# Gates of the prompt's HGRN group: worked out on the projection's tiles instead of in the recurrence's stage

## What is computed

```python
q = silu(q_raw)
log_f = logaddexp(log1p(-lb) + log_sigmoid(f_raw), log(max(lb, 1e-30)))
k = (1 - lb) * sigmoid(-f_raw)
# in chunks, per head, with the state S (64 x 64):
b = cumsum(log_f, axis=time)
attn[t, s] = sum_k q[t, k] * k[s, k] * exp(b[t, k] - b[s, k])      # s <= t
o = attn @ v + (q * exp(b)) @ S
S = exp(b_last)[:, None] * S + (k * exp(b_last - b)).T @ v
out = rms(o) * gain * silu(g_raw)
```

## Time and profile before

| what | value |
|---|---|
| three runs | 4513.45, 4522.64, 4520.75 us, median 4520.75 |
| span of the profiled execution | 4510.9 us |
| least time of a run beside that span | 4513.45 us, 2.55 more |
| TensorE busy | 3762.7 us, 83% |
| VectorE busy | 1959.3 us, 43% |
| ScalarE busy | 1491.7 us, 33% |
| GpSimd busy | 588.2 us, 13% |

### The profile page before, as it was taken

The page is one execution under the profiler, slowest core; times in us unless marked ns, Lnnn a source line. Parts: engine busy times, 40 slices in busy tenths (PEclk is TensorE's granted clock), DMA queues, the critical chain, the costliest instruction groups (busy, mean ns, idle before and its releaser), DMA issues. The chain is left out here.

```text
span 4510.9 us, 50016 instructions
## 1 busy us (share of the span) xinstructions
PE 3762.7 (83%) x18532; PEld 2697.6 (60%) x18532; DVE 1959.3 (43%) x2982; ACT 1491.7 (33%) x2438; POOL 588.2 (13%) x908
## 2 busy tenths in 40 slices
PE   8999965899995664577559986769999999999997
PEld 6778843655562552342324444458788788788875
DVE  4122135877764776332213325533453443443333
ACT  3122123344444544121102214332432343343232
POOL 2001001354555000212010100000000000000000
PEclk9999965999998677687579987789999999999998
DMA  4233222111111001635153302643343233333222
GB/s 148 88 98 121 77 58 67 49 45 31 43 29 66 6 29 59 212 121 180 40 170 103 100 28 69 216 158 94 108 135 103 100 118 118 108 112 103 75 75 77
DMA packets 260783, 421.46 MB, mean 93 GB/s; under 512 B 48291, under 2 KB 150034, under 8 KB 259090
## 3 DMA queue, kind: packets, MB, share of 16 engines
q1 hardware_dynamic: 216054, 293.06, 20.3%
q0 software_dynamic: 35248, 119.86, 8.1%
q10 hardware_dynamic: 9248, 5.46, 0.4%
HBM read 335.89 MB, written 84.50 MB: 93 GB/s over the span
## 5 line engine op out<-in xcount | busy, mean ns | idle before, releaser
L2970 PE MATMUL ff_p<-ff_h,ff_wl 128*128 128x512 f32 x1024 | 403.1, 394 | 30.6 <-DVE ff_wl L3178 23.5
L3178 DVE TENSOR_TENSOR ff_wl<-ff_w_raw,ff_w 128x2048 fp32r<-128x2048 f32 x128 | 293.4, 2292 | 309.9 <-ACT ff_w L3066 309.0
L3031 PE MATMUL ff_p<-ff_w,ff_yl 128*128 128x512 f32 x1024 | 404.1, 395 | 11.3 <-DVE ff_yl L3188 9.6
L3031 PE MATMUL ff_p<-ff_wl,ff_yh 128*128 128x512 f32 x1024 | 401.2, 392 | 0.0
L2970 PE MATMUL ff_p<-ff_hl,ff_w 128*128 128x512 f32 x1024 | 400.8, 391 | 0.0
L3031 PE MATMUL ff_p<-ff_w,ff_yh 128*128 128x512 f32 x1024 | 400.7, 391 | 0.0
L2970 PE MATMUL ff_p<-ff_h,ff_w 128*128 128x512 f32 x1024 | 400.7, 391 | 0.0
L1490 ACT ACTIVATE att_e<-att_p 128x512 f32<-128x512 f32 (+3 forms) x432 | 205.1, 509 | 311.5 <-PE att_p L1378 308.2
L3066 ACT ACTIVATE ff_w<-ff_w_raw 128x2048 fp32r<-128x2048 f32 x128 | 244.6, 1911 | 150.5 <-PE ff_p L3031 113.0
L1542 DVE TENSOR_REDUCE att_mx<-att_p 128x1 f32<-128x512 f32 (+3 forms) x432 | 230.0, 571 | 85.4 <-PE att_p L1409 60.7
L3188 DVE TENSOR_TENSOR ff_yl<-ff_y,ff_yh 128x512 fp32r<-128x512 f32 x256 | 171.4, 689 | 199.6 <-ACT ff_yh L3080 199.6
(11 more groups left out here) (726 smaller groups left out, 7068.0 us busy)
## 6 DMA issues: line engine op xcount, KB each, us to landing
ff_w_raw<-in_w_ff SPq DMA_DIRECT2D x128, 1024.0 KB, 5.3
att_raw<-scratch_feat SPq DMA_DIRECT2D x72, 256.0 KB, 4.2
scratch_feat<-proj_f SPq DMA_DIRECT2D x68, 256.0 KB, 2.0
smp_fox_kv<-in_cache_fox_kv SPq DMA_DIRECT2D x64, 256.0 KB, 5.4
smp_fox_kv<-in_cache_fox_kv POOLq DMA_DIRECT2D x64, 256.0 KB, 5.7
proj_w_raw<-in_w_in POOLq DMA_DIRECT2D x24, 512.0 KB, 4.1
proj_w_raw<-in_w_in POOLq DMA_DIRECT2D x40, 256.0 KB, 4.0
proj_x<-in_x_prompt POOLq DMA_DIRECT2D x16, 512.0 KB, 4.3
```

What stands on the lines that cost most here:

```text
L2970: last = mm(p[:, bank, :], lhs(a, c), b[:, c, :], start=(c == 0 and a is wl), stop=(c == KC - 1 and a is w and b is h))
L3031: last = mm(bank, a[:, v % NY, cols], b[:, U % 2, o:o + 512], start=(q == 0 and s == 0 and a is yl), stop=(q == UB - 1 and s == 3 and a is ...
L3178: v_.tensor_tensor(wl[:, U % 2, :], w_raw[:, U % 2, :], w[:, U % 2, :].bitcast(F32), ALU.subtract).then_inc(w_lo, 1)
```

## The change

The gate work of the prompt moves from the HGRN stage into the projection. Each evicted tile of q, f and g goes through it while it lies in `f`: `gate_first` and `gate_second` on ScalarE, `gate_logs` and `gate_make` on VectorE, the latter two steps one unit later. A tile of f is stored twice, as running sums in a new scratch tensor `hgrn_b` and as k in `feat`; q and g are stored as gated rows. The lower bounds are made in the projection's first units. `squares` gives its place to the new tiles; the squares now go into `xn`, so `norm` waits for an earlier turn. In the HGRN stage the gates go, `b` becomes a ring of four blocks and is loaded, ahead of the gated rows. `Steps` and `lower_bounds` only move up in the file. The diff, cut to the core:

```diff
--- before.py
+++ after.py
@@ stage_project, tiles
-        squares = r.sb("squares", [P, D])
+        ga, gb, once = r.sb("ga", [P, GA, TB]), r.sb("gb", [P, 2, TB]), r.sb("once", [P, TB])
...
@@ SyncE
+            def store_gated(u):
...
+                sp.wait_ge(g_made, n + 1)
+                if what == "f":
+                    sp.dma_start(S["hgrn_b"][c * P:(c + 1) * P, at], f[:, f_use[u] % 4, :]).then_inc(f_stored[f_use[u] % 4], 16)
+                    sp.dma_start(S["feat"][R_HF + c * P:R_HF + (c + 1) * P, at], ga[:, n % GA, :]).then_inc(k_stored[n % GA], 16)
+                else:
+                    row = {"q": R_HQ, "g": R_HG}[what] + c * P
+                    sp.dma_start(S["feat"][row:row + P, at], f[:, f_use[u] % 4, :]).then_inc(f_stored[f_use[u] % 4], 16)
...
-                elif kind == "feat":
+                elif kind == "feat" and u not in gates:
...
                 if u and u - 1 in tr_use:
                     store_turned(u - 1)
+                if u - 1 in gates:
+                    store_gated(u - 1)
@@ ScalarE
+                    act.wait_ge(turned, n - 1)
-                s.activation(squares[0:rows, :], x[0:rows, n % 3, :], ACT.Square, accum_out=ss[0:rows, k]).then_inc(ss_done, 1)
+                s.activation(xn[0:rows, n % 2, :], x[0:rows, n % 3, :], ACT.Square, accum_out=ss[0:rows, k]).then_inc(ss_done, 1)
...
+            def gate_first(u):
+                n, what, c = gates[u]
+                act.wait_ge(out_done, u + 1)
+                if n >= GA:
+                    act.wait_ge(g_made, n - GA + 1)
+                    act.wait_ge(k_stored[n % GA], k_before(n))
+                a = ga[:, n % GA, :]
+                gstep(s.activation(a, f[:, f_use[u] % 4, :], ACT.Abs))
+                gstep(s.activation(a, a, ACT.Exp, scale=-1.0))
+                s.activation(a, a, ACT.Ln, bias=1.0).then_inc(g_first, 1)
+
+            def gate_second(u):
+                n, what, c = gates[u]
+                a, t = ga[:, n % GA, :], f[:, f_use[u] % 4, :]
+                act.wait_ge(g_logs, n + 1)
+                if what == "f":
+                    gstep(s.activation(t, t, ACT.Abs))
+                    gstep(s.activation(t, t, ACT.Exp, scale=-1.0))
+                    gstep(s.activation(t, t, ACT.Ln, bias=1.0))
+                s.activation(a, a, ACT.Exp).then_inc(g_second, 1)
...
                 out(u)
...
+                if u - 1 in gates:
+                    gate_second(u - 1)
+                if u in gates:
+                    gate_first(u)
@@ VectorE
+            def gate_logs(u):
...
+                dve.wait_ge(g_first, n + 1)
+                gstep(v.scalar_tensor_tensor(out=a, in0=t, scalar=0.0, in1=a, op0=ALU.min, op1=ALU.subtract))
+                if what == "f":
+                    gstep(v.tensor_scalar(gb[:, c, :], a, lb["ln_om"][:, c:c + 1], None, ALU.add))
+                    gstep(v.tensor_tensor(a, a, t, ALU.subtract))
+                    gstep(v.tensor_scalar(t, gb[:, c, :], lb["ln_lb"][:, c:c + 1], None, ALU.subtract))
+                dve.sem_inc(g_logs, 1)
+            def gate_make(u):
...
+                dve.wait_ge(g_second, n + 1)
+                if what == "q":
+                    gstep(v.tensor_tensor(t, t, a, ALU.mult))
+                elif what == "g":
+                    gstep(v.scalar_tensor_tensor(out=t, in0=t, scalar=ggain[:, c:c + 1], in1=a, op0=ALU.mult, op1=ALU.mult))
+                else:
+                    v.tensor_scalar(a, a, lb["one_minus"][:, c:c + 1], None, ALU.mult)
+                    gstep(v.scalar_tensor_tensor(out=t, in0=gb[:, c, :], scalar=lb["ln_lb"][:, c:c + 1], in1=t, op0=ALU.max,
+                                                 op1=ALU.add))
+                    gstep(v.tensor_tensor_scan(t, once[:], t, 0.0, ALU.mult, ALU.add))
+                dve.sem_inc(g_made, 1)
...
+                if u - 1 in gates:
+                    gate_make(u - 1)
+                if u in gates:
+                    gate_logs(u)
@@ stage_hgrn
-        b, eb = r.sb("b", [P, 2, 2, TB]), r.sb("eb", [P, 2, 2, TB])
+        b, eb = r.sb("b", [P, 4, 2, TB]), r.sb("eb", [P, 2, 2, TB])
...
+                sp.dma_start(b[:, k % 4, :, :], S["hgrn_b"][:, at].rearrange("(c p) t -> p c t", p=P)).then_inc(b_loaded[k % 4], 16)
...
-            def gate_sigmoids(k):
...
-            def gate_forget(k):
...
-                act.wait_ge(scanned, k + 1)
+                act.wait_ge(b_loaded[k % 4], 16 * (k // 4 + 1))
...
-            def gate_logs(k):
...
-            def gate_scan(k):
...
+                dve.wait_ge(b_loaded[(j // PER) % 4], 16 * (j // PER // 4 + 1))
...
+                dve.wait_ge(z_loaded[k % 4], 48 * (k // 4 + 1))
```

More of the change, by code:

```diff
@@ L175, in _, with __init__, __call__, closed @@
             nc.vector.memset(K["pairones"][HD:P, HD:P], 1.0)
+class Steps:
+    def __init__(self, engine, sem, i=0, per=0):
+        self.engine, self.sem, self.start, self.per, self.n = engine, sem, i * per, per, 0
+    def __call__(self, instruction):
+        self.n += 1
+        instruction.then_inc(self.sem, 1)
+        self.engine.wait_ge(self.sem, self.start + self.n)
+    def closed(self, instruction, passed):
+        self(instruction)
+        self.engine.sem_inc(passed, 1)
+    def end(self):
+        assert self.per == self.n, (self.per, self.n)
 HALF = L // 2
@@ L199, with lower_bounds @@
 PROJ_TURN = {0: ((0, R_FK, P), (P, R_FK + P, P)), 1: ((256, R_CMP, P), (384, R_KS, HD))}
+def lower_bounds(nc, step, low, lb):
+    v = nc.vector
+    return [
+        lambda: step(v.tensor_tensor(lb["shift"][:], low[:], low[:], ALU.subtract)),
+        lambda: step(v.reciprocal(lb["inv"][:], lb["exp"][:])),
+        lambda: step(v.tensor_tensor(lb["soft"][:], lb["exp"][:], lb["inv"][:], ALU.mult)),
+        lambda: step(v.tensor_tensor(lb["lb"][:], lb["soft"][:], lb["soft"][:], ALU.subtract)),
+        lambda: step(v.tensor_scalar(lb["one_minus"][:], lb["lb"][:], -1.0, 1.0, ALU.mult, ALU.add)),
+        lambda: step(v.tensor_single_scalar(lb["floored"][:], lb["lb"][:], 1e-30, ALU.max)),
+    ]
+LN2_60 = 60 * 0.6931471805599453
+GATED = {R_HQ + P * c: ("q", c) for c in range(2)} | {R_HF + P * c: ("f", c) for c in range(2)} | {
+    R_HG + P * c: ("g", c) for c in range(2)}
 def proj_units():
@@ L282, in stage_project, with k_before @@
         sm_stored = r.sems("sm_stored", 2)
+        g_consts, bounds_dve, bounds_act, gate_dve, gate_act = (r.sem(n) for n in (
+            "g_consts", "bounds_dve", "bounds_act", "gate_dve", "gate_act"))
+        g_first, g_logs, g_second, g_made, k_stored = (
+            *(r.sem(n) for n in ("g_first", "g_logs", "g_second", "g_made")), r.sems("k_stored", GA))
         block = r.block()
+        gates = {}
+        for u, (hf, g, kind, a, b) in enumerate(units):
+            if kind == "feat" and PROJ_ROWS[g][a][0] in GATED:
+                gates[u] = (len(gates), *GATED[PROJ_ROWS[g][a][0]])
+        def k_before(n):
+            return 16 * sum(kind == "f" and m % GA == n % GA and m < n for m, kind, _ in gates.values())
         z_use, f_use, zs_use, tr_use, fs_use, sm_use = {}, {}, {}, {}, {}, {}
@@ L430, in _ @@
                     store_turned(u - 1)
+                if u - 1 in gates:
+                    store_gated(u - 1)
+            for k in range(GA):
+                sp.wait_ge(k_stored[k], 16 * sum(kind == "f" and n % GA == k for n, kind, _ in gates.values()))
             for k in range(3):
@@ L616, in _ @@
                     finish_small(u)
+                if u == 1:
+                    dve.wait_ge(g_consts, 32)
+                    low_bounds[0]()
+                    dve.sem_inc(bounds_dve, 1)
+                    ones = once[:].rearrange("p (n t) -> p n t", t=P)
+                    v.memset(ones[:, :, 1:P], 1.0)
+                    v.memset(ones[:, :, 0:1], 0.0)
+                if u == 3:
+                    dve.wait_ge(bounds_act, 1)
+                    for bound in low_bounds[1:]:
+                        bound()
+                    dve.sem_inc(bounds_dve, 1)
+                if u == 5:
+                    dve.wait_ge(bounds_act, 2)
+                    gstep(v.tensor_scalar(lb["ln_lb"][:], lb["ln_lb"][:], LN2_60, None, ALU.subtract))
+                if u - 1 in gates:
+                    gate_make(u - 1)
+                if u in gates:
+                    gate_logs(u)
             for u in (NU - 2, NU - 1):
@@ L723, in _ @@
             turn_out(NU - 1)
-class Steps:
-    def __init__(self, engine, sem, i=0, per=0):
-        self.engine, self.sem, self.start, self.per, self.n = engine, sem, i * per, per, 0
-    def __call__(self, instruction):
-        self.n += 1
-        instruction.then_inc(self.sem, 1)
-        self.engine.wait_ge(self.sem, self.start + self.n)
-    def closed(self, instruction, passed):
-        self(instruction)
-        self.engine.sem_inc(passed, 1)
-    def end(self):
-        assert self.per == self.n, (self.per, self.n)
 def split(v, step, x, high, low):
```

134 lines of the change are left out of this document (31 added, 103 removed).

## The result

Four runs of the changed kernel took 4417.04 to 4428.64 us, median 4424.22, against 4519.56 for four of the kernel before: a ratio of 0.978, 95% interval 0.977 to 0.980, some 95 us less. The forecast was 4430 us in a range of 4412 to 4463. The profiled execution spans 4415.4 us, 95.5 less than the one before.

What follows compares the result with a forecast made beforehand. It took TensorE to bound the projection and a chain of waits across engines, no single engine, the HGRN stage. Opening 30.7 plus chunks 60.3, projection 0, gave 91.0 us less: 4430 us, range 4412 to 4463.

Steps and rivals of the forecast that it cites:

- The opening: Start of the HGRN stage: without block 0's gates the first factors start earlier, a gain of 30.7 us.
- the overlap of VectorE and GpSimd: HGRN opening: VectorE's differences slowed beside GpSimd's selects, 5.6 of eight done by 1432.9, cutting the gain from 32.4 to 30.7.
- the first rival: HGRN opening: GpSimd's selects wait for differences too; opening gain 29.0, total 89.3, 4431.5 us; chance 0.36.
- the sum without contention: HGRN opening undisturbed: exponentials end at 1435.4, masks last at 1436.05, a gain of 32.4 us.
- The chunks: HGRN chunks: without later gates, 13 steps of 11.87 us take 154.3 against 214.6, a gain of 60.3 us.
- free step: HGRN chunk step without gate work of the next block; three taken, 11.90, 11.41 and 12.3, mean 11.87 us.
- The round trip: HGRN chunk step: VectorE, ScalarE, TensorE, VectorE, with the turned keys' copy behind the exponentials; free steps 11.90 or 11.41 us.
- The projection: Input projection: 24 gated tiles hide in ScalarE's waits, cost 0 us, ends 0 and 3; lag about 2.3 us.
- TensorE's clock: Rival for the HGRN chunks: lower clock makes steps 13.65 us, chunk gain 37.2, 4455 to 4458 us; chance 0.14.
- the thirteen: HGRN steps from the third chunk's closing difference to the sixteenth's: 214.6 us before, 154.3 forecast.
- The ring of f tiles: Rival in the projection: four f slots freed too late, beyond 21.8 us, expose the gates, 4564 us; chance 0.03.
- The sum: Whole kernel: opening 30.7 plus chunks 60.3 give a gain of 91.0 us.

Runs made afterwards that it cites:

- the ring of three: Changed kernel with keys' copy before exponentials, three exponent tiles, differences one chunk further ahead, key tile cleared by VectorE; ratio 0.975 to the kernel before.
- the filler: Changed kernel with six identity products per chunk added where TensorE waits for the copied keys; ratio 0.979 to the kernel before.

## Why the prediction was right

*The opening.* Forecast 30.7, measured 31.4. The load was put at 4.3 us and took 4.39. The step that was mis-sized is the overlap of VectorE and GpSimd: 5.6 differences in place of eight until the selects end. The first eight differences took 3.12 us (1429.10 to 1432.22) against 2.85 of the next eight, and the selects 6.33 us in place of 5.83. So VectorE lost 0.3 us where I had priced 2.3 (1433.7 in place of 1431.4), and GpSimd 0.5 where the first rival had 3.3. Both took a little longer, neither by whole instructions. The exponentials were then done by 1436.1 and the masks came last, as the sum without contention had it, only 0.9 later: GpSimd began 0.4 later and lost 0.5. That the number came so near is in part luck: the exponentials, which my sum had last at 1437.7, were early, and the masks, which it had ready at 1436.05, were late. With the clearing moved to VectorE and the wait for the masks put behind the first factors, in the ring of three, these start 11.42 us after the stage's first load in place of 12.27.

The Trainium skill, "SBUF — State Buffer", section "Who interferes with whom", has VectorE with two SBUF inputs and a reading GpSimd instruction exclude each other. The prediction had worked that out as 2.3 us on VectorE's side or 3.3 on GpSimd's; these rows show 0.3 and 0.5, so they agree with it in that both sides pay, not in the amount.

*The chunks.* Forecast 11.87 a step and 60.3 us, measured 11.71 and 62.4. The mean of three had been taken over one free step that TensorE lengthened, and of those there were fewer, two in thirteen. The kernel before had seven steps without gate work among its thirteen, 11.37 to 11.90 long; their mean, 11.63, was the nearer forecast. The round trip was named rightly: the keys' copy, moved, took 1.2 us from it.

*The projection.* Next to 0 us, as forecast (the HGRN stage begins 0.4 us later), with a lag of up to 1.8 us in the first half and 3.1 in the second for 2.3. But the reason given for it, that TensorE feels a late eviction only from 15.7 us on, is wrong: at units that it turns itself it feels one from 4.8 us on. The gates fit because two f tiles are followed by units in which ScalarE catches up, before or nearly before such a unit; the margin was a third of what I thought.

*The rivals.* GpSimd did wait, but for 0.5 us. TensorE's clock took two or three steps of thirteen, 2 to 4 us by the filler, not the whole chunk; what the thirteen hold above 13 x 11.37, from the clock and all else, is 4.4 us in this execution and 6.5 in the second. Its full price appears only in steps shorter than the changed kernel's. The ring of f tiles shows in no row of TensorE's waits.

*The sum.* 95.5 us between the profiled spans against 91.0: 0.7 of the 4.5 from the opening, 2.1 from the chunks, 1.6 behind the sixteenth chunk, which is less than executions differ by.

## What to carry to other kernels

Work inside a latency-bound chain of waits costs up to its full length (VectorE's gates 43.4 us for 43.1 of work; ScalarE's, part of which fell into its waits, 32.7 for 42.6), and is free in a stage where its engine sits waiting for another; look for both in the rows of idle time, not in the shares of busy time. Room for late work in a pipelined stage is set by the unit whose result the leading engine itself takes up next, not by the depth of its ring. After shortening a chain, look at what the leading engine's new, shorter waits do to its clock: filling a wait of 1 us per chunk took 1 us from each of three chunks here. Then look at the whole stage, too: it became only 0.4 us shorter.

## What the runs showed of the hardware that I had not expected

In three chunks of 10.16 us, each with one wait of 1.01 us, TensorE's granted clock was 0.83, and with products of no use in that wait it was 1.00. In the ring of three it stayed at 1.00 for two chunks with a wait of 1.62 us each and fell behind the third. The Trainium skill, "TensorE: Matmul & The Clock Gate", section "HAM oscillation — how this bites in real kernels", tells of the clock swinging between its two levels where matmuls come in bursts between waits for loads; here the waits are for VectorE and far shorter than the bursts, and the clock swings all the same.

VectorE and GpSimd, both reading SBUF, took 0.3 and 0.5 us longer over 4.7 us of overlap (in the ring of three the selects took 6.31 us, too), much less than the sum of 1.57 us in place of 0.69 had led me to expect.
